# Streaming both halves of a split fp32 operand through one 512-column matmul

## The chip, the cores and the metric

One core of one Trainium2 chip runs the whole program. The metric is device time in microseconds of that core, as the median of several executions of one compiled kernel.

## What is computed

The reference takes 256 tokens of width 2048 in fp32 through one large block (three attention branches with gates, then a convolutional feed-forward layer) and two more mixers (gated linear attention, latent attention). Nearly all of the arithmetic is in products of the token activations with large weight matrices that are read once:

```python
proj = h @ w_in                                   # 2048 x (6 x 1024 + ... + 3 x 2048)
merged = (gates[:, :, 0] * (o_sb @ w_branch[0]) + gates[:, :, 1] * (o_dsa @ w_branch[1])
          + gates[:, :, 2] * (o_mem @ w_branch[2]))
x = x + merged @ w_out
u = _causal_dwconv(h2 @ w_up, conv_w, conv_b)     # 2048 x 11008
x = x + (silu(g) * val) @ w_down                  # 5504 x 2048
# second block: the same kind of products, each followed by
x = x + rms_norm(y, g_post)
```

## The kernel before, in words

TensorE has a fast fp32 format (fp32r) that keeps fewer bits than fp32. To get fp32 accuracy each operand is split into a high part (rounded) and a low part (the rest), and a product is three matmuls that accumulate: high x high, high x low, low x high. The fourth product is left out.

**Phases.** The projections are 38 phases in a fixed order (class Phase, L44; list at L200). A phase has blocks of 256 output columns, and a block has 1 to 4 tiles of weights; a tile is 4 (in one place 3) slices of 128 rows by 256 columns, 512 KB. There are 836 tiles. The kinds: "fm" keeps weights still and streams the 256 tokens, so that the output has features on partitions; "tm" keeps the activations of 128 tokens still and streams 256 weight columns; "kv" (16 blocks) does one half each way. Three phases have narrow blocks of one block each, "tm" with 72, 16 and 64 columns (kiwi, decay, krope). The phases qrope, qnope0, qnope1, kv0 and kv1 have one tile in a block, all others two or more.

**Engines.** For each tile SyncE issues the load into one of RING = 4 places of `weight_raw`; ScalarE copies it to `weight_hi` (split_hi, L1087, instruction L1092); VectorE subtracts to make `weight_lo` (split_lo, L1630, instruction L1628, the line of the helper that records every tensor-tensor operation); TensorE runs the 24 matmuls of the tile (project, L589, instruction L628) and signals `tile_used`. ScalarE splits tile t + 4 once tile t is used, so weights are ready some tiles ahead.

**PSUM.** `blk` (L295) has PSUM_RING = 2 places of two banks; a block uses columns 0 to 255 of each bank. TensorE may start block b + 2 when `block_out` says that block b has been taken out. Who takes it out: ScalarE for rows_to (L1119), chunks_to (L1133), gate_tanh (L1139, tanh straight from PSUM) and y_out (L1542); VectorE for scaled_to (L1705, times 1/rms), branch (L1873, times the gate), add_to_x (L2030), conv_scale (L2050) and the kv output (L2273). Each engine's queue is in order: per tile ScalarE does split_hi, then an output, then `mid` and `side` work (softmax, norms, convolution) that is placed by tile index; VectorE does its output first, then split_lo, then `mid` and `side`.

**After an "up" phase** the last block goes through VectorE (conv_scale), ScalarE and VectorE (taps, L1436, L2067, L2072), ScalarE (silu, L1441), VectorE (product), ScalarE (L1445, high part) and VectorE (low part `h_lo`); the "down" phase that follows needs that last chunk in its last tile of the first block: the fourth tile in down0 and down1, the third in down2.

Of the kernel before, what the change touches and what calls it, by code (L numbers as in the profile page):

```python
# [25 lines left out]
P = 128  # L26
ALU = mybir.AluOpType
ACT = mybir.ActivationFunctionType
# [15 lines left out]
class Phase:  # L44


    def __init__(self, name, kind, blocks, ktiles, cols, src):
        self.name, self.kind, self.blocks, self.ktiles = name, kind, blocks, ktiles
        self.cols, self.src = cols, src
        self.bt = len(ktiles)  # L50
        self.n = blocks * self.bt

        self.period = lcm(PSUM_RING * self.bt, RING)


class Plan:


    def __init__(self, phases):
# [3 lines left out]
        b = 0  # L63
        for ph in phases:
            ph.t0, ph.b0 = len(self.shape), b
# [51 lines left out]
S = 256  # L117
# [42 lines left out]
def build_program(nc, x, mem, positions, attn_norm, mem_norm, w_in, b_gate, dsa_q_norm, dsa_k_norm,  # L160
# [33 lines left out]
    def qrope_src(b, kt):  # L194
# [6 lines left out]
        Phase("memk", "tm", 4, K16, TC, cols_from(w_mem_kv[0], 0, K16)),  # L201
        Phase("memv", "tm", 4, K16, TC, cols_from(w_mem_kv[0], W, K16)),
        Phase("qm", "tm", 4, K16, TC, cols_from(win, 6 * W, K16)),
        Phase("gate2", "fm", 8, K16, TC, cols_from(win, GATE0 + 2 * D, K16)),
        Phase("branch2", "fm", 8, K8, TC, cols_from(w_branch[0, 2], 0, K8)),
        Phase("sbqk", "fm", 8, K16, TC, cols_from(win, 0, K16)),
        Phase("sbv", "tm", 4, K16, TC, cols_from(win, 2 * W, K16)),
        Phase("gate0", "fm", 8, K16, TC, cols_from(win, GATE0, K16)),
        Phase("branch0", "fm", 8, K8, TC, cols_from(w_branch[0, 0], 0, K8)),
        Phase("qi", "tm", 2, K16, TC, cols_from(win, 7 * W, K16)),  # L210
        Phase("kiwi", "tm", 1, K16, ID + IH, cols_from(win, 7 * W + IH * ID, K16, ID + IH)),
        Phase("qb", "tm", 4, K16, TC, cols_from(win, 3 * W, K16)),
        Phase("kb", "tm", 4, K16, TC, cols_from(win, 4 * W, K16)),
        Phase("vb", "tm", 4, K16, TC, cols_from(win, 5 * W, K16)),
        Phase("gate1", "fm", 8, K16, TC, cols_from(win, GATE0 + D, K16)),
        Phase("branch1", "fm", 8, K8, TC, cols_from(w_branch[0, 1], 0, K8)),
        Phase("wout", "fm", 8, K16, TC, cols_from(w_out[0], 0, K16)),
    ]
    FFN = [(0, 16), (16, 16), (32, KF - 32)]
    for f, (c0, nf) in enumerate(FFN):  # L220
# [3 lines left out]
            Phase(f"down{f}", "fm", 8, kts, TC, cols_from(down[f], 0, kts)),  # L224
# [3 lines left out]
        Phase("decay", "tm", 1, K16, DECAY_RANK, cols_from(gla_w_in, 3 * D, K16, DECAY_RANK)),  # L228
        Phase("glav", "tm", 8, K16, TC, cols_from(gla_w_in, D, K16)),
# [3 lines left out]
        Phase("krope", "tm", 1, K16, LR, cols_from(mla_w_in, 2 * LRANK, K16, LR)),  # L233
# [27 lines left out]
    with ExitStack() as ctx:  # L261
# [11 lines left out]
        h_hi, h_lo = (sb(n, [P, KD, S], F32R) for n in ("h_hi", "h_lo"))  # L273
        u_hi, u_lo = (sb(n, [P, KD, S], F32R) for n in ("u_hi", "u_lo"))
# [52 lines left out]
        probs, probsT = area(T, 4, TRI), area(T + 4 * TRI, 4, TRI)  # L327

# [56 lines left out]
        block_out = sem("block_out")  # L385
# [202 lines left out]
        def _(pe):  # L588
            def project(ph, x_hi, x_lo, side=None, x_wait=None, lead=None):  # L589

                def tile(j, i):
# [12 lines left out]
                    hi, lo = weight_hi[:, t % RING], weight_lo[:, t % RING]  # L604
                    for c in range(2):
                        tok = slice(c * P, c * P + P)
                        if ph.kind == "fm":
                            o = blk[:, b % PSUM_RING, c, 0:S]
                            ops = [(w[:, k, c * P:c * P + P], v[:, TK * kt + k, :])
                                   for k in range(nk) for w, v in ((hi, x_hi), (hi, x_lo), (lo, x_hi))]  # L610
                            groups = [(o, ops)]
                        elif ph.kind == "tm":
                            o = blk[:, b % PSUM_RING, c, 0:ph.cols]
                            ops = [(v[:, TK * kt + k, tok], w[:, k, 0:ph.cols])
                                   for k in range(nk) for w, v in ((hi, x_hi), (lo, x_hi), (hi, x_lo))]
                            groups = [(o, ops)]
                        elif c == 0:
                            groups = [(blk[:, b % PSUM_RING, 0, 0:S],
                                       [(w[:, k, 0:P], v[:, k, :])
# [1709 lines left out]
```

## Time and profile before

| | us |
|---|---|
| median of 3 runs (2691.66 to 2693.73) | 2693.29 |
| span of the profiled execution | 2691.4 |
| TensorE matmul busy | 2643.3 (98%) |
| TensorE weight load busy | 2610.1 (97%) |
| VectorE busy | 1535.4 (57%) |
| ScalarE busy | 1239.8 (46%) |
| GpSimd busy | 115.3 (4%) |
| HBM read | 439.02 MB, 164 GB/s |

The span runs from the first to the last instruction of the program in one profiled execution. Matmul spans in the trace overlap each other, and their ends are modelled; the distance from one start to the next is what an instruction costs. Busy shares are averages over stages that differ.

### The profile page before, as it was taken

The numbers are of one execution on the slowest core, as the hardware profiler recorded it, in microseconds if no ns is written. First come the engines' busy times: TensorE is split into PE (matmuls) and PEld (weight loads), VectorE is DVE, ScalarE is ACT, GpSimd is POOL, SyncE is SP. The second block draws the span as 40 slices with busy tenths as digits, with TensorE's granted clock in tenths as the row PEclk, the third lists the DMA queues.
The fourth block names the chain that finished last, engine by engine and source line by source line (L and its number), as shares of the span: only waits on it lengthen the run. The fifth ranks groups of instructions, "written<-read, shape, count | busy, mean of one in ns | idle before, by whom it ended". The sixth has DMA issues, their size and how long they took to land.

```text
span 2691.4 us, 53007 instructions
## 1 busy us (share of the span) xinstructions
PE 2643.3 (98%) x21308; PEld 2610.1 (97%) x21308; DVE 1535.4 (57%) x1829; ACT 1239.8 (46%) x1551; POOL 115.3 (4%) x82
## 2 busy tenths in 40 slices
PE   7999999999999999999999999999999997999998
PEld 7999999999999999999999999999999997999897
DVE  6644544554684566666466646675254846565454
ACT  6544344543444444554345434453344444334353
POOL 3000000100000001000000000010001111000001
PEclk9999999998999999999999999999899998899998
DMA  6554555454555655665566556556354553444443
GB/s 202 181 180 141 181 186 180 145 174 141 160 179 154 201 175 185 181 181 185 183 180 183 183 181 183 179 177 180 112 165 133 167 186 111 125 119 141 117 165 109
DMA packets 545539, 443.49 MB, mean 165 GB/s; under 512 B 31241, under 2 KB 542753, under 8 KB 544866
## 3 DMA queue, kind: packets, MB, share of 16 engines
q1 hardware_dynamic: 545186, 441.00, 53.5%
q8 instruction: 120, 1.97, 0.3%
q0 software_dynamic: 192, 0.18, 0.1%
q14 instruction: 41, 0.34, 0.0%
HBM read 439.02 MB, written 2.10 MB: 164 GB/s over the span
## 4 chain that ended last, share of the span: by engine, by line
PE 95%; DVE 3%; ACT 1%; DMA 0%; issue 0%; POOL 0%; SPq 0%; DVEq 0%; ACTq 0%
PE blk L628 88%; PE pa L881 1%; DVE arena L1628 1%; PE pa L692 1%; DVE u_lo L1675 1%; DVE weight_lo L1628 0%; DMA weight_raw<-in_w_mem_kv_dram 0%; PE pa L972 0%; DVE xT L1628 0%; ACT weight_hi L1092 0%; POOL arena L570 0%; PE pa L683 0%; PE pa L654 0%; DVE arena L2185 0%; PE pa L644 0%
## 5 line engine op out<-in xcount | busy, mean ns | idle before, releaser
L1628 DVE TENSOR_TENSOR weight_lo<-weight_raw,weight_hi 128x1024 fp32r<-128x1024 f32 (+2 forms) x836 | 1018.5, 1222 | 973.5 <-ACT weight_hi L1092 971.4
L1092 ACT ACTIVATE weight_hi<-weight_raw 128x1024 fp32r<-128x1024 f32 (+2 forms) x836 | 871.2, 1045 | 1283.5 <-PE blk L628 1251.2
L628 PE MATMUL blk<-u_hi,weight_hi 128*128 128x256 f32 x2656 | 756.8, 285 | 16.5 <-DVE u_lo L1675 14.4
L628 PE MATMUL blk<-u_lo,weight_hi 128*128 128x256 f32 x2656 | 754.4, 284 | 0.0
L628 PE MATMUL blk<-u_hi,weight_lo 128*128 128x256 f32 x2656 | 754.3, 284 | 0.0
L628 PE MATMUL blk<-h_hi,weight_hi 128*128 128x256 f32 x2608 | 741.9, 284 | 1.8 <-DVE h_lo L1628 1.8
L628 PE MATMUL blk<-h_hi,weight_lo 128*128 128x256 f32 x2608 | 738.7, 283 | 0.0
L628 PE MATMUL blk<-h_lo,weight_hi 128*128 128x256 f32 x2608 | 738.6, 283 | 0.0
L628 PEld LDWEIGHTS blk<-u_hi,weight_hi 128*128 128x128 f32 x2656 | 512.6, 193 | 19.3 <-issue 16.7
L628 PEld LDWEIGHTS blk<-u_lo,weight_hi 128*128 128x128 f32 x2656 | 512.8, 193 | 0.1
L628 PEld LDWEIGHTS blk<-u_hi,weight_lo 128*128 128x128 f32 x2656 | 512.7, 193 | 0.0
L628 PEld LDWEIGHTS blk<-h_hi,weight_hi 128*128 128x128 f32 x2608 | 501.3, 192 | 2.1 <-issue 2.0
L628 PEld LDWEIGHTS blk<-h_lo,weight_hi 128*128 128x128 f32 x2608 | 501.4, 192 | 0.1
L628 PEld LDWEIGHTS blk<-h_hi,weight_lo 128*128 128x128 f32 x2608 | 501.2, 192 | 0.0
L628 PE MATMUL blk<-weight_lo,h_hi 128*128 128x256 f32 (+2 forms) x896 | 257.0, 287 | 0.0
L628 PE MATMUL blk<-weight_hi,h_lo 128*128 128x256 f32 (+2 forms) x896 | 256.8, 287 | 0.0
L628 PE MATMUL blk<-weight_hi,h_hi 128*128 128x256 f32 (+2 forms) x896 | 256.6, 286 | 0.0
L628 PEld LDWEIGHTS blk<-weight_hi,h_hi 128*128 128x128 f32 x896 | 176.8, 197 | 0.5 <-DVE weight_lo L1628 0.3
L628 PEld LDWEIGHTS blk<-weight_hi,h_lo 128*128 128x128 f32 x896 | 176.8, 197 | 0.0
L628 PEld LDWEIGHTS blk<-weight_lo,h_hi 128*128 128x128 f32 x896 | 176.7, 197 | 0.0
L628 PE MATMUL blk<-weight_hi,u_hi 128*128 128x256 f32 (+2 forms) x576 | 170.5, 296 | 4.7 <-DVE weight_lo L1628 4.7
L628 PE MATMUL blk<-weight_lo,u_hi 128*128 128x256 f32 (+2 forms) x576 | 168.8, 293 | 0.0
(244 smaller groups left out, 1991.7 us busy)
## 6 DMA issues: line engine op xcount, KB each, us to landing
weight_raw<-in_w_in_dram SPq DMA_DIRECT2D x216, 512.0 KB, 3.4
weight_raw<-in_w_up_dram SPq DMA_DIRECT2D x344, 256.0 KB, 3.1
weight_raw<-in_l_gla_w_in_dram SPq DMA_DIRECT2D x96, 512.0 KB, 3.7
weight_raw<-in_w_down_dram SPq DMA_DIRECT2D x80, 512.0 KB, 3.3
weight_raw<-in_w_branch_dram SPq DMA_DIRECT2D x48, 512.0 KB, 3.3
weight_raw<-in_l_mla_w_in_dram SPq DMA_DIRECT2D x48, 512.0 KB, 3.7
weight_raw<-in_w_mem_kv_dram SPq DMA_DIRECT2D x32, 512.0 KB, 4.3
weight_raw<-in_w_out_dram SPq DMA_DIRECT2D x32, 512.0 KB, 3.3
```

What stands on the lines that cost most here:

```text
L628: mm = nc.tensor.matmul(o, lhsT, rhs, start=(kt == 0 and m == 0), stop=(kt == ph.bt - 1 and m == len(ops) - 1))
L692: nc.tensor.matmul(pa[:, h, 0:S], values[:, 0, v], probs_T[:, h, 0:S], start=True, stop=False)
L881: mm = nc.tensor.matmul(pa[:, h, o], lhsT, rhs, start=(m == 0), stop=(m == len(ops) - 1))
L1092: nc.scalar.activation(weight_hi[:, r, 0:nk, 0:cols], weight_raw[:, r, 0:nk, 0:cols], ACT.Copy).then_inc(hi_made, 1)
L1628: return nc.vector.tensor_tensor(out_, a, b, op)
L1675: nc.vector.scalar_tensor_tensor(x_lo[:, c, :], src[:, c, :], col(gain, c), x_hi[:, c, :].bitcast(F32), ALU.mult, ALU.subtract).then_inc(N ...
```

## The change

Phases with more than one tile in a block become "merged". The two halves of the streamed operand lie side by side (`weight[P, RING, 2, TK, TC]`, `h` and `u` as `[P, 2, KD, S]`), and one matmul streams both: 512 columns in two runs of 256, into columns 0 to 511 of a bank. A second matmul, with the low part of the other operand still, streams the high half into columns 0 to 255. So three matmuls of 256 columns become one of 512 and one of 256. The bank ends with two partial results in its two halves, which have to be added: ScalarE copies the upper half to SBUF ("lift", signal block_lifted), then VectorE adds the lower half from PSUM ("join", signal block_joined or block_out). Where the old output did arithmetic straight from PSUM, it now follows as its own instruction on SBUF data. `add_to_x` needs no lift: VectorE adds both halves in two instructions. Phases with one tile in a block keep their three matmuls.

```diff
+        self.merged = self.bt > 1
+        self.lift = self.merged and evict != "add"
+        self.join = self.merged and evict != "copy"
...
-        weight_hi = sb("weight_hi", [P, RING, TK, TC], F32R)
-        weight_lo = sb("weight_lo", [P, RING, TK, TC], F32R)
+        weight = sb("weight", [P, RING, 2, TK, TC], F32R)
+        weight_hi, weight_lo = weight[:, :, 0], weight[:, :, 1]
...
+            def weights_still(o, w, v):
+                n = v.shape[-1]
+                if o.shape[-1] == n:
+                    return [(o, w[:, 0, :], v[:, 0, :]), (o, w[:, 0, :], v[:, 1, :]), (o, w[:, 1, :], v[:, 0, :])]
+                return [(o, w[:, 0, :], v), (o[:, 0:n], w[:, 1, :], v[:, 0, :])]
+            def weights_move(o, v, w):
+                n = w.shape[-1]
+                if o.shape[-1] == n:
+                    return [(o, v[:, 0, :], w[:, 0, :]), (o, v[:, 0, :], w[:, 1, :]), (o, v[:, 1, :], w[:, 0, :])]
+                return [(o, v[:, 0, :], w), (o[:, 0:n], v[:, 1, :], w[:, 0, :])]
...
+                    halves = 1 + ph.merged
-                            o = blk[:, b % PSUM_RING, c, 0:S]
+                            o = blk[:, b % PSUM_RING, c, 0:halves * S]
...
 # ScalarE, in tile(), after split_hi
+                        lift(b, r).then_inc(block_lifted if ph.merged else block_out, 1)
+                        if final is not None:
+                            act.wait_ge(block_joined, b + (ph.j0 + 1))
+                            final(b).then_inc(block_out, 1)
...
+            def tanh_of_gate(g):
+                def go(b):
+                    for c in range(2):
+                        v = gates[:, bass.ds(b * 2 + c, 1), :]
+                        ins = nc.scalar.activation(v, v, ACT.Tanh, bias=col("b_gate", b * 2 + (g * KD + c)), scale=0.5)
...
 # VectorE, in tile(), after split_lo
+                    if j % ph.bt == ph.bt - 1 and join is not None:
+                        dve.wait_ge(block_lifted, b + (ph.l0 + 1))
+                        join(ph, b, r)
...
+            def chunks_joined(dst, done):
+                def go(ph, b, r):
+                    v = dst[:, bass.ds(b * 2, 2), :]
+                    tt(v, v, blk[:, r, :, 0:S], ALU.add).then_inc(done, 1)
...
 # VectorE, branch(n)
+                    v = m if n == 0 else branch_part[:, r]
+                    tt(v, v, blk[:, r, :, 0:S], ALU.add).then_inc(block_joined, 1)
+                    dve.wait_ge(block_joined, b + (ph.j0 + 1))
+                    tt(v, v, g, ALU.mult).then_inc(block_out, 1)
...
 # VectorE, add_to_x
+                    tt(v, v, blk[:, r, :, 0:S], ALU.add).then_inc(block_joined, 1)
+                    dve.wait_ge(block_joined, b + (ph.j0 + 1))
+                    tt(v, v, blk[:, r, :, S:2 * S], ALU.add).then_inc(block_out, 1)
...
 # VectorE, conv_scale
+                    v = conv_in[:, r]
+                    tt(v, v, blk[:, r, :, 0:S], ALU.add).then_inc(block_joined, 1)
+                    dve.wait_ge(block_joined, b + (ph.j0 + 1))
+                    tt(v, v, RSTD["ffn"].unsqueeze(1).to_broadcast([P, 2, S]), ALU.mult).then_inc(block_out, 1)
...
 # ScalarE, y_out
-                    unit_norm(n, b, blk[:, r, :, 0:S], 2)
+                    unit_norm(n, b, y[:, 2 * b:2 * b + 2, :], 2)
+                    norm_at(act, n, "sq", b + 1)
```

## Rows read from the trace of the kernel before

**Rows 1.** The page: busy time of TensorE, and the chain that ended last

```profile
PE 2643.3 (98%) x21308; PEld 2610.1 (97%) x21308; DVE 1535.4 (57%) x1829; ACT 1239.8 (46%) x1551; POOL 115.3 (4%) x82
PE 95%; DVE 3%; ACT 1%; DMA 0%; issue 0%; POOL 0%; SPq 0%; DVEq 0%; ACTq 0%
```

**Rows 2.** Timeline of TensorE, us 1000 to 1004: start us, duration us, instruction

```profile
1000.08 0.28 PE L628 MATMUL blk<-h_hi,weight_hi 128*128 128x256 f32 x1
1000.20 0.28 PE L628 MATMUL blk<-h_lo,weight_hi 128*128 128x256 f32 x1
...
1003.92 0.28 PE L628 MATMUL blk<-h_hi,weight_lo 128*128 128x256 f32 x1
```

**Rows 3.** Groups by shape, TensorE: instruction, count, busy us, mean ns, idle before

```profile
L628 PE MATMUL blk<-u_hi,weight_hi 128*128 128x256 f32 x2656 | 756.8, 285 | 16.5 <-DVE u_lo L1675 14.4 <-DVE weight_lo L1628 2.0
L628 PE MATMUL blk<-h_hi,weight_hi 128*128 128x256 f32 x2608 | 741.9, 284 | 1.8 <-DVE h_lo L1628 1.8
L628 PE MATMUL blk<-weight_hi,h_hi 128*128 128x256 f32 x736 | 210.7, 286 | 0.0
L628 PE MATMUL blk<-weight_hi,u_hi 128*128 128x256 f32 x512 | 149.8, 293 | 4.7 <-DVE weight_lo L1628 4.7
L628 PE MATMUL blk<-weight_hi,h_lo 128*128 128x72 f32 x32 | 11.8, 368 | 0.0
```

**Rows 4.** Timeline of TensorE in a kv block: from 256 to 128 columns

```profile
2357.63 0.22 PE L628 MATMUL blk<-weight_hi,h_hi 128*128 128x128 f32 x1
2357.69 0.28 PE L628 MATMUL blk<-weight_lo,h_hi 128*128 128x128 f32 x1
2357.81 0.27 PE L628 MATMUL blk<-weight_hi,h_lo 128*128 128x128 f32 x1
```

**Rows 5.** Timeline of TensorE in decay: 16 columns

```profile
1908.83 0.26 PE L628 MATMUL blk<-weight_hi,u_lo 128*128 128x16 f32 x1
1908.94 0.26 PE L628 MATMUL blk<-weight_hi,u_hi 128*128 128x16 f32 x1
```

**Rows 6.** Timeline of weight loads of plain fp32 matmuls with 512 columns

```profile
1927.32 0.18 PEld L948 LDWEIGHTS pa<-arena 17*128 17x128 f32 x1 [0.24 <-issue]
...
1928.61 0.18 PEld L948 LDWEIGHTS pa<-arena 17*128 17x128 f32 x1 [0.24 <-issue]
```

**Rows 7.** Low clock: timeline of TensorE, then the kiwi stage among the windows by stage (us, busy of PE, PEld, DVE, ACT, POOL, granted clock)

```profile
1931.53 0.41 PE L628 MATMUL blk<-weight_lo,u_hi 128*128 128x256 f32 x1
1931.74 0.41 PE L628 MATMUL blk<-weight_hi,u_lo 128*128 128x256 f32 x1
...
646.20:663.40 17.20, 17.20 (x98) 17.20 (x97) 4.13 (x4) 4.10 (x5) 0.00 (x0) 0.60 0.46 140
```

**Rows 8.** Groups by shape, VectorE and ScalarE: the splits and outputs from PSUM

```profile
L1628 DVE TENSOR_TENSOR weight_lo<-weight_raw,weight_hi 128x1024 fp32r<-128x1024 f32 x816 | 1006.6, 1237 | 953.5 <-ACT weight_hi L1092 951.4
L1628 DVE TENSOR_TENSOR arena<-blk,rstd 128x512 f32<-128x512 f32 x67 | 46.2, 689 | 41.7 <-PE blk L628 39.9 <-ACT small L1177 1.3 <-ACT rstd L1175 0.6
...
L1092 ACT ACTIVATE weight_hi<-weight_raw 128x1024 fp32r<-128x1024 f32 x816 | 860.1, 1057 | 1252.0 <-PE blk L628 1219.7 <-issue 15.8 <-DMA weight_raw<-in_w_mem_kv_dram 7.5
L1136 ACT ACTIVATE arena<-blk 128x512 f32 x8 | 4.7, 582 | 0.0
```

**Rows 9.** Windows by stage: kb, then branch1 (columns as in the window of rows 7)

```profile
719.20:766.90 47.70, 47.70 (x402) 47.70 (x401) 43.61 (x96) 23.55 (x25) 0.00 (x0) 1.00 0.59 179
...
920.60:966.70 46.10, 46.10 (x386) 46.10 (x385) 33.51 (x35) 20.54 (x21) 0.00 (x0) 1.00 0.63 202
```

**Rows 10.** Timeline at the end of up2: VectorE, then TensorE

```profile
1743.10 0.69 DVE L1628 TENSOR_TENSOR arena<-blk,rstd 128x512 f32<-128x512 f32 x1 [0.88 <-PE blk L628]
1745.33 0.42 DVE L1628 TENSOR_TENSOR arena<-arena 128x256 f32<-128x256 f32 x1
...
1750.60 0.36 PE L628 MATMUL blk<-h_hi,weight_hi 128*128 128x256 f32 x1 [1.78 <-DVE h_lo L1628]
```

**Rows 11.** Windows by stage: glagate, the stretch of the output norm (columns as in rows 7)

```profile
2083.00:2117.00 34.00, 32.34 (x268) 32.06 (x266) 28.58 (x29) 15.75 (x17) 6.66 (x2) 1.00 0.47 140
```

More of the change, by code:

```diff
@@ L62, in __init__ @@
         self.end_of = []
-        b = 0
+        b = lifts = joins = 0
         for ph in phases:
-            ph.t0, ph.b0 = len(self.shape), b
+            ph.t0, ph.b0, ph.l0, ph.j0 = len(self.shape), b, lifts, joins
+            lifts += ph.blocks * ph.lift
+            joins += ph.blocks * ph.join
             for j in range(ph.n):
@@ L612, in tile @@
                         elif ph.kind == "tm":
[L613 to L616, printed above, removed]
+                            o = blk[:, b % PSUM_RING, c, 0:halves * ph.cols]
+                            groups = [[op for k in range(nk) for op in weights_move(
+                                o, x[:, :, TK * kt + k, tok], w[:, :, k, 0:ph.cols])]]
@@ L626, in tile @@
-                        for o, ops in groups:
-                            for m, (lhsT, rhs) in enumerate(ops):
-                                mm = nc.tensor.matmul(o, lhsT, rhs, start=(kt == 0 and m == 0),
+                            o = blk[:, b % PSUM_RING, 0, 0:S]
+                            groups = [[op for k in range(nk) for op in weights_still(
+                                o, w[:, :, k, 0:P], x[:, :, k, :])]]
+                        else:
+                            groups = []
+                            for q in range(NT):
+                                o = blk[:, b % PSUM_RING, 1, q * P:(q + 1) * P]
+                                groups.append([op for k in range(nk) for op in weights_move(
+                                    o, x[:, :, k, q * P:q * P + P], w[:, :, k, P:2 * P])])
@@ L629, in tile @@
+                        for ops in groups:
+                            for m, (to, lhsT, rhs) in enumerate(ops):
+                                mm = nc.tensor.matmul(to, lhsT, rhs, start=(kt == 0 and m == 0),
                                                       stop=(kt == ph.bt - 1 and m == len(ops) - 1))
@@ L1403, in round_merged @@
                                      ACT.Copy).then_inc(merged_hi, 1)
[L1406 removed]
+            project(PH["branch1"], to_branch_part(2), side=lambda j: round_merged(j // 4 - 1) if j % 4 == 0 and j > 0 else None)
             round_merged(3)
@@ L2018, in side_dsa @@
                     split_out(ATT["dsa"], g, 4)
-            project(PH["gate1"], side=side_dsa, mid=gates_of(PH["gate1"]))
+            project(PH["gate1"], join=chunks_joined(gates, block_joined), side=side_dsa, mid=gates_of(PH["gate1"]))
             dve.wait_ge(gate_done, 24)
```

320 lines of the change are left out of this document (173 added, 147 removed).

## The prediction, made before the changed kernel ran

> **What bounds the kernel now.** First the page's busy rows and the chain that ended last [rows 1]: TensorE is busy for 98% of the span and holds 95% of the chain, VectorE 57% and ScalarE 46% of the span. So time is won or lost in what a matmul costs and in the few places where TensorE waits. Busy shares say nothing on what a matmul costs, because the spans overlap; the timeline does. In steady state starts are (1003.92 - 1000.08) / 32 = 0.120 us apart [rows 2]. Next question: is that 0.120 set by the columns, by the weight load, or by something fixed per matmul? The change keeps the columns (3 x 256 = 512 + 256) and takes away one weight load and one matmul of three, so it gains only what is not columns.
>
> Four rows bear on it. (a) With 16 columns the starts are 0.11 apart [rows 5]: a weight load by itself costs 0.11. (b) Going from 256 to 128 columns, the first narrow matmul gives way after 0.06, the next after 0.12, then 0.11: the first found its weights loaded and cost its columns, the later ones wait for loads [rows 4]. So 128 columns cost 0.06 and 256 cost 0.12, which looks like a rate (0.47 ns a column), where the clock of 2.4 GHz would give 0.053 and 0.107. (c) A plain fp32 matmul with 512 columns has starts (1928.61 - 1927.32) / 3 = 0.430 apart, four times 0.1075, with its load hidden [rows 6]: there a long stream carries almost nothing beside its columns. (d) At the low clock, 1.2 GHz, 256 columns cost 0.21, which is 256 / 1.2 and nothing else [rows 7]: nothing can be gained in those stretches.
>
> **The change part by part.**
>
> Wide triples. The groups by shape [rows 3] count 2656 + 2608 + 736 + 512 = 6512 triples with 256 columns. Of these qrope has 32, qnope0 and qnope1 64, kv0 and kv1 64, which keep three matmuls: 6352 change. About a hundred lie in stretches at the low clock, which follow narrow stages; I count 6250. Each costs 3 x 0.120 = 0.360 now. Afterwards the 256-column matmul is followed by the load for the 512-column one, as tight as today: 0.120. The 512-column matmul is not in the trace. From below: 0.215, half of (c), if its excess vanishes because a load of 0.11 ends in its first half. From above: 0.240, twice 0.120, if fp32r streams at the rate that (b) suggests. A fixed excess of 0.0133 per matmul would give 0.2267. The rows of its own kind of operand speak for the upper end, the load that is hidden for the lower; I take the middle, 0.228, so a triple costs 0.348 and saves 0.012. That is 6250 x 0.012 = 75 us, between 0 and 156.
>
> By the Trainium skill, page "TensorE: Matmul & The Clock Gate", section "Back-to-back issue gap", an isolated matmul costs its columns at 2.4 GHz plus 2.5 ns. By that rule a triple would cost 0.216 + 0.109 = 0.325 and the sum would lose 219 us. The trace disagrees already for what is there: 0.120 where the rule gives 0.109 [rows 2].
>
> Narrow triples. Three stages with 72, 16 and 64 columns have 32 triples each (one of them in [rows 3]). They are bound by loads, 0.11 at full clock and 0.21 at low [rows 5, 7], and each triple loses a load: 96 x 0.11 = 11 to 96 x 0.21 = 20 us. The kiwi stage averages 17.20 / 96 = 0.179 [rows 7], so 96 x 0.179 = 17, and with a little for a clock that may recover sooner as the array is fed more columns per load, 18 us.
>
> Lift and join. Per merged block ScalarE reads 128x512 from PSUM, 0.58, and VectorE adds 128x512, 0.69 [rows 8]; outputs that did arithmetic from PSUM keep their instruction, now from SBUF. There are 216 merged blocks: at most 150 us more for VectorE (57% to about 63%), less for ScalarE, which did the copy in many phases already. That is hidden as long as three covers hold. First, the PSUM ring: from the end of a block ScalarE splits (1.06) and lifts (0.58), VectorE joins (0.69) and works on (0.69), about 3.3 with signals, against a block time of 4 x 8 x 0.348 = 11.1, or 5.6 in the branch phases with two tiles. Second, VectorE's time. The kb stage is the fullest, 43.61 of 47.70 [rows 9]; four joins make it 46.5 against a stage of 46.1, and the excess of 0.4 is taken up by the weights that are split ahead. branch1 has 33.51 of 46.10 [rows 9]; eight joins make 39.0 of 44.5. Third, ScalarE: where it must wait for block_joined (gates, glaout, mlaout), the next split_hi is queued behind, and TensorE waits for that only after some three tiles, 8 us.
>
> Where cover is gone. At the end of an "up" phase the last chunk takes 1750.60 - 1743.10 = 7.5 [rows 10]. VectorE's product starts at 1745.33; now the join (0.69), the scaling (0.69) and a signal stand between split_lo and it: 1.5 later, 9.0. down0 and down1 have three tiles of cover, 3 x 2.78 = 8.3: 0.7 stall each. down2 has two, 5.6: its stall of 1.78 grows by about 1.5. Sum 3. In glagate VectorE is busy 28.58 of 34 [rows 11] and TensorE waits for weight_lo at its end, so twelve faster tiles gain nothing there (1.2) and three joins with their waits (2.6) come on top: 4. At the ends of glaout and mlaout TensorE waits for the norm of the last block, which now comes after a lift and a join: 2 x 1.3 = 2.6. For the gates and the start I add 2.4. Together 12, between 5 and 25.
>
> **Sum.** 2691.4 - 75 - 18 + 12 = 2610 for the span. The median of the runs is 1.9 above this span, so 2612.
>
> **The rivals.**
>
> Rate-bound stream: fp32r moves at 0.47 ns a column, 512 cost 0.240, a triple 0.360 as before. For it speaks that 128 cost 0.06 and 256 cost 0.12 [rows 2, 4]; against it that plain fp32 runs at its clock [rows 6]. Only narrow stages gain: -18 + 12, 2687.
>
> Hidden load: the excess comes from the load that ends together with the stream, and a long stream has none. 0.215 + 0.120 = 0.335: -156 - 18 + 14, 2533. For it rows 6, against it that the first 128-column matmul, with its weights ready, still cost 0.06 and not 0.053 [rows 4].
>
> No excess in either: the plain fp32 rate throughout, 0.215 + 0.109 = 0.325: -219 - 18 + 16, 2472. For it rows 6, against it rows 2. This is what the page's rule amounts to.
>
> Slower: reading two runs of 256 that lie apart costs extra at the seam, in every 512-column matmul. The point from which this decides is (18 - 12) / 6250 = 0.001 above 0.240, so 0.241; at 0.250 the kernel is at 2691.4 + 62 - 6 + 1.9 = 2749. No row shows a stream in two runs; that the reads are far ahead of the array speaks against it.
>
> It does not do what it says: the 512-column instruction is carried out as two of 256, each with its load. Then three matmuls a slice remain and only the additions stay: 2705. The plain fp32 matmuls with 512 columns stand whole in the trace [rows 6].
>
> **How the numbers follow.** Forecast 0.42 (its own range 2580 to 2660, from 0.220 to 0.235 for the long matmul); rate-bound 0.19; hidden load 0.20; no excess 0.08; seam 0.08; split in two 0.03. The range 2530 to 2692 holds the first three, 0.81. A measurement of this kernel can tell some 0.2%, 5.4 us, from no change. Faster: 0.42 + 0.20 + 0.08 + 0.11 of the rate-bound case, which lies at the bound, 0.81. Same: 0.08, the rest of that case. Slower: 0.08 + 0.03 = 0.11.
>
> **What would show it.** Starts in the timeline of a steady stage: 0.228 after a long matmul and 0.120 after a short one; any other split of the sum names the rival. L628 or its successor should have 6448 x 2 + 288 x 3 = 13 760 matmuls instead of 20 208. Weight loads should be busy for clearly less than 97%. The copies of 0.58 and additions of 0.69 should appear 216 times at most, with no wait of TensorE for block_out in steady stages. A stall of about 3.4 at the start of down2 and small ones in down0 and down1 should appear. The prediction is wrong if the long matmul leaves 0.220 to 0.235, or if TensorE waits in steady stages for outputs or weights, which would mean that ScalarE's wait for the join holds back the splits.

## The result and the profile after

The changed kernel takes 2644.85 us (median, 2642.61 to 2647.79) against 2692.47 for the kernel before on the same chip: ratio 0.9825, 95% interval 0.9811 to 0.9838, some 48 us faster. The forecast was 2612, a gain of 81; somewhat over half of it came (47.6). The profiled execution spans 2646.0. First the page, busy times and the chain that ended last, the lines that answer to [rows 1].

```profile
PE 2570.5 (97%) x14860; PEld 2239.3 (85%) x14860; DVE 1666.9 (63%) x2063; ACT 1310.4 (50%) x1686; POOL 107.4 (4%) x82
PE 86%; DVE 7%; ACT 4%; issue 1%; POOL 1%; DMA 1%; SPq 0%; DVEq 0%; ACTq 0%; POOLq 0%
```

TensorE still holds most of the chain, but its part fell from 95% to 86%, and VectorE and ScalarE together rose from 4% to 11%. Weight loads went from 97% to 85%. So the time is no longer only in what a matmul costs. Next the groups by shape, TensorE first, then the new copy, the new addition and the tanh that follows it, to be read against [rows 3, 8].

```profile
L648 PE MATMUL blk<-u,weight 128*128 128x512 f32 x2656 | 944.0, 401 | 17.9 <-DVE u L1752 14.5 <-DVE weight L1678 2.9 <-ACT xT L1172 0.4
...
L648 PE MATMUL blk<-u,weight 128*128 128x256 f32 x2656 | 746.6, 281 | 0.0
...
L1678 DVE TENSOR_TENSOR arena<-arena,blk 128x512 f32<-128x512 f32 x99 | 67.3, 680 | 9.4 <-ACT arena L1164 9.4
...
L1172 ACT ACTIVATE xT<-xT,vec 128x256 f32<-128x256 f32 x48 | 21.8, 502 | 34.9 <-DVE xT L1678 34.7
...
L1164 ACT ACTIVATE xT<-blk 128x512 f32<-128x512 f32 x24 | 13.9, 580 | 0.0
```

A copy is 0.580 and an addition 0.680, as costed. New is the idle time in front of the tanh: ScalarE sat 34.7 us, in 24 blocks, waiting for VectorE's addition.

What a triple (the matmuls that make one product of a slice) costs can't be read from the 401 ns, because spans overlap. ScalarE shows it: its weight split in each tile waits for TensorE to have used a tile, so in a steady stage splits are one tile (8 triples) apart. Two steady stretches of the same kernel, splits of ScalarE between 1520 and 1700 us, then between 1300 and 1480 (count, first and last start), and last the kernel before between 1300 and 1480:

```profile
L1112 ACT ACTIVATE weight<-weight_raw x65: 1042/1060/1062, 1521.4 to 1698.9; 128x1024 fp32r<-128x1024 f32 x65
...
L1112 ACT ACTIVATE weight<-weight_raw x63: 1043/1062/1063, 1300.6 to 1475.8; 128x1024 fp32r<-128x1024 f32 x63
```
```profile
L1092 ACT ACTIVATE weight_hi<-weight_raw x63: 1042/1058/1060, 1299.6 to 1478.1; 128x1024 fp32r<-128x1024 f32 x63
```

(1698.9 - 1521.4) / 64 = 2.773 us a tile, 0.3467 a triple; and (1475.8 - 1300.6) / 62 = 2.826, 0.3532 a triple. Nothing else differs: same shapes, same weights' size, no wait. The kernel before has one period, (1478.1 - 1299.6) / 62 = 2.88, 8 x 0.360. Over all steady triples of the changed kernel's trace the starts give 0.3507, with 0.2346 after a long matmul and 0.1161 after a short one. Then the windows of three stages: kiwi, gate1 and glagate (us, busy of PE, PEld, DVE, ACT, POOL, granted clock, DMA), against [rows 7] for the first, and gate1 in the kernel before.

```profile
638.65:645.71 7.06, 7.06 (x66) 7.06 (x65) 4.09 (x5) 4.11 (x5) 0.00 (x0) 1.00 0.68 192
791.87:904.83 112.96, 105.94 (x603) 92.68 (x602) 57.81 (x62) 56.05 (x91) 0.00 (x0) 0.97 0.53 158
1990.30:2102.64 112.34, 106.50 (x586) 92.03 (x585) 77.33 (x73) 56.11 (x59) 18.30 (x7) 0.97 0.51 150
```
```profile
814.74:920.64 105.90, 105.55 (x859) 104.53 (x858) 53.02 (x55) 52.24 (x84) 0.00 (x0) 1.00 0.54 169
```

kiwi went from 17.20 to 7.06 and its granted clock from 0.60 to 1.00. gate1 got longer, 105.9 to 113.0, although its matmuls got cheaper: TensorE idles for 7.0 us in it, where it idled for 0.4 before. What it waits for stands in the waits of TensorE over the whole trace (us in total, times, longest); the kernel before has 6.8 for the first of these lines, 0.9 for the line that is L712 here, 0.8 for L690, 1.8 for `h`, and no wait of 0.8 or more for L721, L833, L703 and L787.

```profile
PE blk L648 <- DVE weight L1678: 7.5, 5, 2.9
...
PE pa L712 <- ACT arena L1333: 7.0, 4, 3.1
...
PE pa L721 <- DVE arena L1678: 4.5, 2, 2.5
...
PE pa L690 <- ACT arena L1209: 4.1, 2, 2.8
PE blk L648 <- DVE h L1678: 4.1, 3, 3.3
PE pa L1017 <- POOL arena L576: 3.0, 1, 3.0
PE pa L833 <- POOL arena L532: 2.1, 1, 2.1
PE pa L703 <- DVE arena L1678: 1.7, 1, 1.7
...
PE pa L787 <- DVE arena L1678: 1.2, 1, 1.2
```

L690 and L1017 are sums for norms, `h` is the start of the down stages, and the other new ones are matmuls of the attention that run beside gate stages. The 7.0 of gate1 are both waits of L721 (4.5), transposes of the probabilities, and one of the four of L712 (2.5), their product with the values; that L712 has 7.0 in the whole trace as well is chance. Waits for weights and for a block's output stayed small: the first line is the start and glagate, where it grew from 1.9 to 2.9, and one output ends a wait, gate1's last tanh by 0.4 in branch1 (the 0.4 on L1172 in the groups above).

### The profile page after: what moved, and what is told of

The parts are those of the page before. It is cut to its first block, busy times and chain, and to the rows that moved or that the text cites. A ratio compares the mean times of both kernels' runs of the same rounds, so it can differ in the third digit from the quotient of the medians.

```text
span 2646.0 us, 40634 instructions
## 1 busy us (share of the span) xinstructions
PE 2570.5 (97%) x14860; PEld 2239.3 (85%) x14860; DVE 1666.9 (63%) x2063; ACT 1310.4 (50%) x1686; POOL 107.4 (4%) x82
## 4 chain that ended last, share of the span: by engine, by line
PE 86%; DVE 7%; ACT 4%; issue 1%; POOL 1%; DMA 1%; SPq 0%; DVEq 0%; ACTq 0%; POOLq 0%
PE blk L648 79%; DVE weight L1678 2%; DVE arena L1678 1%; PE pa L901 1%; ACT weight L1112 1%; ACT arena L1326 1%; PE pa L712 1%; DVE xT L1678 1%; DVE u L1752 1%; DMA weight_raw<-in_w_mem_kv_dram 0%; PE pa L992 0%; DMA weight_raw<-in_w_branch_dram 0%; DVE small L1915 0%; DVE arena L2278 0%; PE pa L703 0%
## 5 line engine op out<-in xcount | busy, mean ns | idle before, releaser
L1678 DVE TENSOR_TENSOR weight<-weight_raw,weight 128x1024 fp32r<-128x1024 f32 (+2 forms) x836 | 1019.5, 1224 | 828.2 <-ACT weight L1112 824.7
L1112 ACT ACTIVATE weight<-weight_raw 128x1024 fp32r<-128x1024 f32 (+2 forms) x836 | 870.4, 1045 | 1033.4 <-PE blk L648 990.6
L648 PE MATMUL blk<-u,weight 128*128 128x512 f32 x5312 | 948.5, 341 | 17.9 <-DVE u L1752 14.5
L648 PEld LDWEIGHTS blk<-u,weight 128*128 128x128 f32 x5312 | 817.2, 190 | 144.0 <-issue 18.0
L648 PE MATMUL blk<-h,weight 128*128 128x512 f32 (+1 forms) x5344 | 929.2, 335 | 4.1 <-DVE h L1678 4.1
L648 PEld LDWEIGHTS blk<-h,weight 128*128 128x128 f32 x5344 | 806.1, 189 | 117.1 <-issue 5.0
L648 PE MATMUL blk<-weight,h 128*128 128x256 f32 (+4 forms) x1952 | 312.1, 321 | 0.0
L648 PEld LDWEIGHTS blk<-weight,h 128*128 128x128 f32 x1952 | 278.4, 190 | 31.7 <-issue 0.3
L648 PE MATMUL blk<-weight,u 128*128 128x512 f32 (+5 forms) x1152 | 210.1, 344 | 4.6 <-DVE weight L1678 4.6
L648 PEld LDWEIGHTS blk<-weight,u 128*128 128x128 f32 x1152 | 181.4, 201 | 29.5 <-DVE weight L1678 5.4
L1475 ACT ACTIVATE arena<-arena,vec 128x256 f32<-128x256 f32 x86 | 46.5, 588 | 0.9 <-DVE arena L1678 0.9
L1172 ACT ACTIVATE xT<-xT,vec 128x256 f32<-128x256 f32 x48 | 21.8, 502 | 34.9 <-DVE xT L1678 34.7
```

Source lines behind the costliest of these rows:

```text
L648: mm = nc.tensor.matmul(to, lhsT, rhs, start=(kt == 0 and m == 0), stop=(kt == ph.bt - 1 and m == len(ops) - 1))
L1112: nc.scalar.activation(weight_hi[:, r, 0:nk, 0:cols], weight_raw[:, r, 0:nk, 0:cols], ACT.Copy).then_inc(hi_made, 1)
L1172: ins = nc.scalar.activation(v, v, ACT.Tanh, bias=col("b_gate", b * 2 + (g * KD + c)), scale=0.5)
L1475: nc.scalar.activation(conv[:, r, c, :], conv_in[:, r, c, :], ACT.Identity, bias=col("conv_b", b + at), scale=col("conv_w2", b + at)).then ...
L1678: return nc.vector.tensor_tensor(out_, a, b, op)
```

## The experiments

The theory at the start (T): the matmuls brought what the two periods say, and the copies and additions cost far more than the 12 us of the sum, because the attention work of ScalarE and VectorE is queued behind their waits for each other. The rival (R): the attention's chains were just hidden before, and a quicker TensorE uncovers them; the additions are innocent.

**Additions alone.** Each wide slice in three matmuls again, everything else as changed (shown for the kind with weights still; the other kind is changed alike).

```diff
-return [(o, w[:, 0, :], v), (o[:, 0:n], w[:, 1, :], v[:, 0, :])]
+return [(o[:, 0:n], w[:, 0, :], v[:, 0, :]), (o[:, n:2 * n], w[:, 0, :], v[:, 1, :]),
+        (o[:, 0:n], w[:, 1, :], v[:, 0, :])]
```

> The changed kernel with each wide slice computed by three matmuls of 256 columns again (high into the lower half, low into the upper half, weight's low part into the lower half); all copies and additions of the two halves stay. Nothing of the computation is left out. Every triple should cost 0.360 as before, so this measures what the copies and additions cost. Theory T (the copies and additions, above all ScalarE's wait for VectorE's addition, hold up the attention work that TensorE waits for; the change gave away some 33 us there): some of it shows already at the old pitch, 2705 to 2725, with TensorE waits of 2 us and more in gate1 behind the probabilities' copy. Rival R (the stages gate0, gate1 and mlagate wait for chains on ScalarE and VectorE that were just hidden before, and a quicker TensorE uncovers them; the additions themselves cost nothing): 2688 to 2700. My prediction's sum, which put 12 us on the additions at the new pitch: 2704.

Measured: 2720.67 us, ratio 1.0106 (1.0089 to 1.0123): the additions cost 28.5 us at the old pitch. That is T, and R's 2688 to 2700 falls. The waits of TensorE show the same lines (here two lines further down) while the matmuls are as slow as before:

```profile
PE pa L714 <- ACT arena L1335: 6.1, 3, 2.9
...
PE pa L723 <- DVE arena L1680: 3.1, 2, 1.8
```

**Matmuls alone.** The matmuls and the layout as changed, no copy and no addition; the outputs keep their old instructions and their old place in the tile, which on VectorE is ahead of its split. The upper half is never added, so one of the three partial products is left out of the result. (The edit is shortened to its sense.)

```diff
-lift(b, r).then_inc(block_lifted if ph.merged else block_out, 1)
+out_of_psum(b, ...).then_inc(block_out, 1)        # reads blk[:, r, :, 0:S]
-dve.wait_ge(block_lifted, b + (ph.l0 + 1))
-join(ph, b, r)
```

> The kernel before with the new matmuls alone: the high and low part of the moving operand stream in one 512-column matmul into the two halves, the outputs read the lower half with the old instructions, and nothing adds the upper half, so the products with the moving operand's low part are left out of the result. It measures what the matmuls alone bring. Theory T (the loss lies in copies and additions): 2692 - 79 = 2613 to 2620, gate1 at 102 to 104 us instead of 113, no new TensorE waits. Rival R (a quicker TensorE uncovers chains that stood just behind it): 2635 to 2645, gate1 at 108 or more. Both expect the two steady periods of 0.347 and 0.353 per triple, since no output instruction touches them; if only one period appears, the two levels come from VectorE's or ScalarE's reads of PSUM.

Measured: 2604.88 us (2596.1 to 2611.08), ratio 0.9666 (0.9640 to 0.9692). The matmuls bring 87.3 us. The window of gate1, and TensorE's wait for the probabilities over the whole trace:

```profile
781.05:884.21 103.16, 102.57 (x604) 90.19 (x603) 52.52 (x54) 51.78 (x84) 0.00 (x0) 1.00 0.58 172
```
```profile
PE pa L712 <- ACT arena L1314: 1.1, 2, 0.6
```

gate1 takes 103.16 with 0.6 us idle, and the wait is 1.1 in place of 7.0. So a quicker TensorE by itself uncovers nearly nothing. That gives 2644.85 - 2604.88 = 40.0 for the additions at the new pitch and 28.5 at the old. "The additions" are here everything that the new outputs bring, copies, additions, waits and their place behind the splits; the runs don't part these. R may keep a small part, some 11 us that arise only where both meet, but this kernel's executions lie 15 us apart, so the 11 is hardly clear of the spread. Both periods, 0.3467 and 0.3533, are in this trace too, so the readers of PSUM don't make them.

Lengths of stages, from a stage's first block matmul to that of the next, in us:

| stage | before | additions alone | matmuls alone | changed | ScalarE's order | both orders |
|---|---|---|---|---|---|---|
| gate2 | 109.4 | 112.5 | 106.6 | 110.6 | 107.1 | 107.8 |
| gate0 | 109.6 | 114.2 | 107.5 | 112.8 | 112.5 | 108.1 |
| gate1 | 105.9 | 111.5 | 103.2 | 113.0 | 109.5 | 106.7 |
| glagate | 110.5 | 113.5 | 110.9 | 112.4 | 111.9 | 112.1 |
| glaout | 103.4 | 106.3 | 101.7 | 103.7 | 102.9 | 102.9 |
| mlagate0 | 70.6 | 71.7 | 69.5 | 71.4 | 71.3 | 71.3 |
| mlagate1 | 71.9 | 75.4 | 71.0 | 75.8 | 74.8 | 75.8 |

Between "matmuls alone" and "changed" the three gate stages lose 4.0 + 5.3 + 9.8 = 19.1 and the two mlagate stages 1.9 + 4.8 = 6.7: most of the 38.3 between the two spans. The timeline of the changed kernel at the end of gate1 (start, duration, engine, instruction, idle before) shows how:

```profile
875.90 1.06 ACT L1112 ACTIVATE weight<-weight_raw 128x1024 fp32r<-128x1024 f32 x1 [5.30 <-PE blk L648]
876.86 0.58 ACT L1164 ACTIVATE xT<-blk 128x512 f32<-128x512 f32 x1
876.99 1.23 DVE L1678 TENSOR_TENSOR weight<-weight_raw,weight 128x1024 fp32r<-128x1024 f32 x1 [3.22 <-ACT weight L1112]
878.13 0.68 DVE L1678 TENSOR_TENSOR xT<-xT,blk 128x512 f32<-128x512 f32 x1
878.85 0.91 ACT L1172 ACTIVATE xT<-xT,vec 128x256 f32<-128x256 f32 x2 [1.40 <-DVE xT L1678]
879.66 1.43 ACT L1333 ACTIVATE arena<-pa 128x1536 f32<-128x1536 f32 x1
...
881.14 1.22 PE L712 MATMUL pa<-arena 128*128 128x256 f32 x2 [2.51 <-ACT arena L1333]
```

ScalarE copies the upper half, waits 1.40 for the addition, which itself stands behind VectorE's split (1.23), does the tanh, and only then copies the probabilities (L1333), for which TensorE has been waiting 2.51. It could have begun after the first copy, at 877.44, and began 2.2 us later. The wait has a tail: the window of TensorE right behind it (us, busy of PE, granted clock, DMA share, GB/s) shows a granted clock of 0.54, that is the lower of the two levels, 1.2 GHz, nearly throughout, after the engine had stood still; the matmuls alone have no such stretch in gate1, whose clock is 1.00. Not every stop has such a tail: the longer one of 3.31 at the start of down2, in the second line, left the clock at 1.00.

```profile
881.20:884.60 3.40, 3.40 (x11) 0.54 0.06 19
1715.50:1722.00 6.50, 3.19 (x19) 1.00 0.04 6
```

**ScalarE's order.** The tile's attention work (`side`) ahead of the wait and the tanh.

```diff
 lift(b, r).then_inc(...)
-if final is not None:
-    act.wait_ge(block_joined, b + (ph.j0 + 1))
-    final(b).then_inc(block_out, 1)
 ... mid, side ...
+if j % ph.bt == ph.bt - 1 and final is not None:
+    act.wait_ge(block_joined, b + (ph.j0 + 1))
+    final(b).then_inc(block_out, 1)
```

> The changed kernel with one step moved on ScalarE: at the end of a gate block the attention work of the tile (exponentials, copies of probabilities) is issued right after the copy of the upper half, and the wait for VectorE's addition and the tanh come last. Nothing of the computation is left out. Theory T (TensorE's new waits in the gate stages come from the attention work queued behind ScalarE's wait for the addition): gate1 goes from 113 to 103 to 106 us, gate0 and gate2 lose 1 to 3 us each, 2645 - 14 = 2631 (2626 to 2636). Rival R (those chains are merely uncovered by a quicker TensorE): moving the step by some 2 us changes less than 5 us, 2640 to 2645. mlagate0, mlagate1 and glagate have no such step and stay as they are under both.

Measured: 2636.01 us (2632.94 to 2646.24), 8.8 less than the changed kernel's median, at the upper end of T's range; the two kernels' executions overlap, so the stages have to decide. gate2 and gate1 lost 3.5 each, gate0 only 0.3, and gate1's 109.5 misses the 103 to 106 that T asked for. In gate1 the wait of L712 for the copy of the probabilities is gone, and the two of L721, behind VectorE, are 4.5 as before. So T holds for ScalarE's own work, and for the rest VectorE's order has to be tried: it issues its part of the attention behind its wait for ScalarE's copy.

**Both orders.** On VectorE `side` now stands ahead of the wait for block_lifted and the addition, where the stage is a gate stage or has no `mid`.

```diff
+if late and side is not None:
+    side(j + i * ph.period)
 if j % ph.bt == ph.bt - 1 and join is not None:
     dve.wait_ge(block_lifted, b + (ph.l0 + 1))
     join(ph, b, r)
 ... mid ...
-if side is not None:
+if not late and side is not None:
     side(j + i * ph.period)
```

> The changed kernel with the attention and gating work of a tile moved ahead of the halves' additions on both engines: ScalarE issues it before it waits for the addition and works on, VectorE issues it before it waits for ScalarE's copy and adds. Nothing of the computation is left out. Theory T (the additions cost time because other work that TensorE waits for is queued behind the two engines' waits for each other): the stages come near those of the matmuls alone, gate2 107, gate0 108 to 110, gate1 103 to 106, mlagate0 70, mlagate1 71 to 73; against 2645 that is 26 us less at most: 2619 to 2630. Rival W (it is the additions' own work on two filled engines, not the order): no better than with ScalarE's order alone, 2634 to 2638.

Measured: 2630.51 us (2622.42 to 2631.56), ratio 0.9762 (0.9748 to 0.9775), just above T's range and below W's. The three gate stages are now 322.6 together, against 336.4 changed and 317.3 with the matmuls alone: order alone gives back 13.8 of the 19.1 (of either number less than 1 is the mix of the two periods). The window of gate1, then what is left of the waits of L721:

```profile
785.30:892.03 106.73, 102.78 (x604) 90.29 (x601) 57.87 (x62) 55.74 (x91) 0.00 (x0) 1.00 0.56 168
```
```profile
PE pa L721 <- DVE arena L1678: 3.8, 2, 2.1
```

Its idle time is 4.0 instead of 7.0, and its clock 1.00 instead of 0.97: with the waits that are left the clock doesn't fall in gate1. The 3.8 are as good as all of those 4.0. For the longer of the two, 2.1, VectorE has the same instructions in the same order before it in both kernels: an addition and the gate's last step for one block, the next tile's split, and only then the scaling of the probabilities. This order inside a tile doesn't give that back, so W fits this rest.

Against the expectation mlagate0 stays at 71.3 and mlagate1 at 75.8. mlagate1's timeline in this kernel shows two engines that wait for each other in another place:

```profile
2503.20 1.22 DVE L1678 TENSOR_TENSOR weight<-weight_raw,weight 128x1024 fp32r<-128x1024 f32 x1
2504.34 0.68 DVE L1678 TENSOR_TENSOR arena<-arena,blk 128x512 f32<-128x512 f32 x1
...
2505.05 0.69 DVE L1678 TENSOR_TENSOR arena<-arena,rstd 128x512 f32<-128x512 f32 x1
...
2505.78 0.64 ACT L1191 ACTIVATE arena<-arena 128x512 f32<-128x512 f32 x1 [3.19 <-DVE arena L1678]
...
2509.16 1.43 ACT L1333 ACTIVATE arena<-pa 128x1536 f32<-128x1536 f32 x1
...
2510.64 1.22 PE L712 MATMUL pa<-arena 128*128 128x256 f32 x2 [3.08 <-ACT arena L1333]
```

Here the silu (L1191), which is itself side work, waits 3.19 for VectorE's addition and scaling, and the copy of the probabilities comes after it. This order of side work doesn't reach that; no other was tried.

**Gate stages in three matmuls.** gate0 to gate2, glagate and both mlagate get `merged = False` and their old output instructions.

```diff
-self.merged = self.bt > 1
+self.merged = self.bt > 1 and evict != "three"
-project(PH["glagate"], join=joined_scaled(g_gate, "pre0"), side=side_gla)
+project(PH["glagate"], scaled_to(g_gate, "pre0"), side=side_gla)
```

> The changed kernel with the stages gate0, gate1, gate2, glagate, mlagate0 and mlagate1 as before the change (three matmuls of 256 columns, old output instructions), everything else changed. Nothing of the computation is left out. By the difference of the stages between the two kernels (gate2 +1.2, gate0 +3.2, gate1 +7.1, glagate +1.9, mlagate0 +0.8, mlagate1 +3.9, which it gives back): 2645 - 18 = 2627 under both theories. If it stays at 2640 or more, the stage table does not add up, and stalls only move to the next stage.

Measured: 2633.52 us; the profiled execution spans 2628.9. The stages are back at 109.4, 110.0, 105.9, 110.5, 70.6 and 71.9, as in the kernel before. The table adds up; the median is 6 above what was expected, and the run that the trace shows 4.

**What sets the period.** Three changes to the matmuls alone, each with one execution, which serve only for the pitch: the first two stream other columns than the product needs, and none adds the upper half. The first streams two neighbouring chunks, so that the 512 columns lie side by side; the second does so with 384; the third lets the short matmul stream both halves too.

```diff
-return [(o, w[:, 0, :], v), (o[:, 0:n], w[:, 1, :], v[:, 0, :])]
+at = (TK * kt + min(k, nk - 2)) * S          # first two: flat is x as one row
+(o[:, 0:512], w[:, 0, k, ...], flat[:, at:at + 512]), (o[:, 0:S], w[:, 1, k, ...], flat[:, at:at + S])
+return [(o, w[:, 0, :], v), (o, w[:, 1, :], v)]          # third
```

> The kernel with the new matmuls alone, in which the 512 streamed columns lie side by side in SBUF (two neighbouring chunks of the high part) instead of in two runs that lie far apart. Result is meaningless: the upper half gets another product, and the last chunk of a tile streams its neighbour's columns; the number and the shapes of the matmuls are the same. No seam cost: a triple stays at 0.347 or 0.353, mean about 0.3505, one time 2596 to 2611. Rival seam (the second period, or the 0.0076 by which the long matmul exceeds 0.2267, comes from the jump between the two runs): only 0.347 or less remains, 2580 to 2590.

> As the one before, with 384 streamed columns in the long matmul instead of 512 (a part of the computation is left out). It tells a fixed excess per matmul from a rate per column: with 256 columns at 0.120 and 512 at 0.2346, fixed means 0.160 + 0.013 = 0.173, a pair at 0.293 to 0.300; 0.47 ns a column means 0.180 and a pair at 0.300 to 0.307. Time: some 6250 x 0.053 = 330 us less than the matmuls alone, 2260 to 2300, unless ScalarE or VectorE become the bound.

> The kernel with the new matmuls alone, in which the matmul with the weight's low part streams both halves too (product of the two low parts comes on top; nothing reads the upper half). All wide matmuls then have 512 columns. Fixed excess of 0.0133: 0.2267 each, a pair at 0.453. Rate of 0.47 ns a column: 0.240 each, a pair at 0.480. If the second steady period comes from the change between long and short matmuls, there should be one pitch only. Time: 2605 + 6250 x 0.103 = 3249 with the fixed excess, 3414 with the rate.

Measured: 2599.45, 2321.42 and 3240.8 us. The splits of ScalarE again, side by side first (two stretches), then 384 columns, then 512 columns in both:

```profile
L1128 ACT ACTIVATE weight<-weight_raw x65: 1042/1060/1062, 1300.0 to 1477.5; 128x1024 fp32r<-128x1024 f32 x65
...
L1128 ACT ACTIVATE weight<-weight_raw x28: 1043/1062/1063, 2060.9 to 2137.2; 128x1024 fp32r<-128x1024 f32 x28
```
```profile
L1128 ACT ACTIVATE weight<-weight_raw x65: 1058/1058/1062, 249.5 to 399.7; 128x1024 fp32r<-128x1024 f32 x65
```
```profile
L1112 ACT ACTIVATE weight<-weight_raw x50: 1059/1061/1062, 1540.7 to 1718.5; 128x1024 fp32r<-128x1024 f32 x50
```

- Side by side: 177.5 / 64 = 2.773 and 76.3 / 27 = 2.826 a tile. Both periods remain, at the same values: the jump between the two runs costs nothing.
- 384 columns: 150.2 / 64 = 2.347 a tile, 0.2934 for a long and a short one. At 2.4 GHz 640 columns are 0.2667; the rest is 2 x 0.0133. All steady stretches of this trace have this one period. (TensorE then waits more for splits, 20.2 us, so the total fell less than expected.)
- 512 in both: 177.8 / 49 = 3.629 a tile, / 16 = 0.2268 each: 512 / 2.4 = 0.2133 and 0.0135. Again one period.

So a matmul with its own weights costs its columns at 2.4 GHz plus a fixed 0.0133, at 256 (0.120) and 512 columns and, in turn with 256, at 384, and the rate of 0.47 ns a column, which would give 0.300 for 384 and 256, is out. On top of it 512 and 256 in turn have a second period, 0.0067 longer.

**Long ones together.** In each half tile the four long matmuls first, then the four short ones, everything else as changed.

```diff
+if ph.merged:
+    groups = [g[0::2] + g[1::2] for g in groups]
 for ops in groups:
```

> The changed kernel with the order of the matmuls inside a half tile changed and nothing else: the four long matmuls first, then the four short ones, instead of long and short in turn. Nothing of the computation is left out. Theory A (each matmul carries a fixed 0.0133, and the second period of 0.3533 is a way in which a strict alternation of long and short can lock; 512 columns alone go at 0.2267 and 256 alone at 0.120): every wide tile goes at 8 x 0.3467 = 2.773 us whatever came before, the mean per triple falls from 0.3507 to 0.347 and the kernel gains 6250 x 0.004 = 25 us, 2620 (2616 to 2626), with less spread between runs. Rival B (the second period belongs to a state of the machine, not to the order of the instructions): two levels per tile remain, 2638 to 2648. Rival C (a change from long to short costs something itself): below 0.3467 per triple, under 2610.

Measured: 2644.34 us (2643.77 to 2652.05), ratio 0.9819 (0.9804 to 0.9834): no gain. The splits in the two stretches where the changed kernel had its two periods:

```profile
L1114 ACT ACTIVATE weight<-weight_raw x64: 1042/1060/1067, 1299.7 to 1476.5; 128x1024 fp32r<-128x1024 f32 x64
...
L1114 ACT ACTIVATE weight<-weight_raw x65: 1042/1060/1067, 1519.3 to 1698.9; 128x1024 fp32r<-128x1024 f32 x65
```

176.8 / 63 = 179.6 / 64 = 2.806, 0.3508 a triple in both. The two periods are gone, so they do hang on the order, against B's reason though the time is B's; but the one in their place is not the 0.3467 of theory A, it lies between them. A's fixed excess therefore doesn't hold for a mixture in any order. What the extra 0.004 consists of stays open.

**Together.** The two orders of side work with the grouped order; then glagate and the mlagate stages in three on top; and that last step with the matmuls in turn.

> The grouped order together with the side work ahead of the additions on both engines. Nothing of the computation is left out. If both gains are independent (theory A above, and 14 us of the side work): 2645 - 25 - 14 = 2606 (2602 to 2612). If the faster tiles only uncover the chains in the attention stages again: 2612 to 2618.

> As the one before, and glagate, mlagate0 and mlagate1 computed in three matmuls of 256 columns with the old output instructions, since these stages took 112.1, 71.3 and 75.8 us with the additions and 110.5, 70.6 and 71.9 without them. Nothing of the computation is left out. Expected 6 us below the one before, 2600 (2595 to 2608); the rival is that their stalls, uncovered, come back elsewhere: equal to the one before.

> The kernel with the side work ahead of the additions on both engines (2630.5), in which glagate, mlagate0 and mlagate1 are computed in three matmuls of 256 columns again with the old output instructions. The matmuls stay in turn, long and short. Nothing of the computation is left out. By the stage table 1.6 + 0.7 + 3.9 = 6 us less: 2624.5 (2617 to 2628, since the steady period is 0.3467 or 0.3533 by chance of where a stage begins). With the grouped order the same step brought 5.0 us. Rival: the grouped order was what made it worth it, then 2630.

Measured: 2632.63, 2627.61 and 2625.54 us (ratio of the last 0.9759, 0.9746 to 0.9772). The step to three brought 5.0 in both settings, as the stages said (6), and the grouped order brought nothing here either (2632.63 against 2630.51), so the gain of 25 on which two of these expectations rested was not there. 2625.54 is the lowest median of a kernel that computes everything, 19 us below the changed one; from 2627.61 it can't be told apart (2621.49 to 2631.95 against 2626.39 to 2631.05).

## Why the prediction was right, and where its sum was off

2644.85 lies in the range and the sign was right; the forecast was 33 too low; the time is inside the forecast's own range of 2580 to 2660. By itself the time says little, since the range of 2530 to 2692 was wide enough for three of the cases; the case is decided by the pitch. Step by step:

- **Bound and count.** Right: only the excess over columns can be gained; 13 760 matmuls on L648; loads at 85%.
- **Wide triples.** 0.012 predicted, 360 - 350.7 = 0.0093 measured, 58 us instead of 75. The 0.228 was the middle between two bounds, not a mechanism that had been argued for; that the fixed excess, which the prediction names with 0.2267, is what the runs show (0.2268 alone; a triple 0.3467 in its better period, below the 0.348 of the sum) and lies next to that middle is in part luck. What was missing is the second period. The sign that was named, 0.228 after a long matmul and 0.120 after a short one, came as 0.2346 and 0.1161, the first just inside its 0.235; only the sum and the runs of one length show what a matmul costs. Its rivals fall by the same rows: rate-bound needs 0.240 for every long one, hidden load 0.215, the seam more for two runs than for one, and split in two would leave the pitch at 0.360. The row that was held against the last one was misread: the program has four plain fp32 matmuls with 512 columns on L948, and the trace has eight records of them, each with its own load, so they do not stand whole, and the 0.430 of [rows 6] is half of one. The pitch and the count decide against it instead. The 0.215 for 512 columns isn't touched by that.
- **The weighed rule.** The Trainium skill, page "TensorE: Matmul & The Clock Gate", section "Back-to-back issue gap", gives columns at 2.4 GHz plus 2.5 ns for an isolated matmul. No run here reaches that with weights that change every matmul: the plus is 13.3 ns at three sizes.
- **Narrow triples.** 18 predicted; kiwi, decay and krope lost 10.2 + 4.7 + 6.3 = 21.2. kiwi shows why a little more: no low clock in it, 1.00 instead of 0.60; krope still has 0.71.
- **FFN ends.** Right for down2, too high for the others. The timeline at the end of up2, to be read against [rows 10]:

```profile
1709.83 5.71 PE L648 MATMUL blk<-h,weight 128*128 128x512 f32 x32
...
1712.26 0.68 DVE L1678 TENSOR_TENSOR arena<-arena,blk 128x512 f32<-128x512 f32 x1
1712.97 0.69 DVE L1678 TENSOR_TENSOR arena<-arena,rstd 128x512 f32<-128x512 f32 x1
1713.58 0.41 DVE L1678 TENSOR_TENSOR arena<-arena 128x256 f32<-128x256 f32 x1
...
1718.85 0.47 PE L648 MATMUL blk<-h,weight 128*128 128x512 f32 x1 [3.31 <-DVE h L1678]
```

  From the block's end to down2's last group 1718.85 - 1709.83 = 9.0, as worked out; the stall is 3.31 against 3.4. The waits for `h` were 1.8 before and are 4.1 now, so down0 and down1 stall for 0.4 each, not 0.7, and the three ends add 2.3 instead of 3.
- **Added stalls.** This is the step that failed: 12 predicted, with a range up to 25, and 40.0 measured (2644.85 - 2604.88), 28.5 of it even at the old pitch. glagate was near: it gained nothing from 256 faster triples (2.4) and came 1.9 longer than before, 4.3 in all against 4. So were the ends of glaout and mlaout, 2.0 and 1.7 longer than with the matmuls alone, against 2.6 for both (from mlaout's last block matmul to the end 23.2 us against 21.5; of the 2.1 by which the stage itself is longer, 1.7 is the second period). The gates had a share in "for the gates and the start 2.4" and took 19.1; both mlagate stages had none and took 6.7. The third cover was argued wrongly: of what is queued behind ScalarE's wait for block_joined the prediction named the next split_hi, which has three tiles of slack. In the same tile, ahead of that, stands `side`, the attention's exponentials and copies, and those have almost none: in the timeline above TensorE had stood for 2.51 before the copy let it go on. The two orders of side work show it by giving 13.8 of the 19.1 back; the other 5.3, and most of what is outside the gates, stay with the additions themselves or weren't taken apart.
- **The other two covers.** They held: in kb, the fullest stage for VectorE (43.61 + 4 x 0.69 is 46.4, not 46.5), TensorE never waited and all its triples run at the longer period, 46.9 in all; in branch1 it waited 0.4 for an output.

The runs of the parts give the sum in two terms: the matmuls alone brought 87.3 where 75 + 18 = 93 were worked out, 6 missing, and the additions took 40.0 where it was 12, 28 too much. Together that is the 33.7 by which the gain fell short (81.3 - 47.6). The 87.3 is 8 more than the triples' 58 and the narrow stages' 21. Between the two traces the gain is 2691.4 - 2607.7 = 83.7, of which the narrow stages have 22.8, so that 3 are left over the triples' 58; the other 4 are that the profiled execution was 4.6 slower than the median of this kernel, whose executions lie 15 us apart.

## What to carry to other kernels

Where a new wait is put into an engine's tile, list everything that the engine issues after it in the same tile, and ask of each who waits for it and how soon: work with the least slack must stand ahead of the wait, even if it is "beside" the main work. A matmul that needs fresh weights has a fixed price beside its columns, so fewer and longer ones pay, by that price and no more; and a stage that already hides a tight chain on the other engines may be better left as it is (glagate and both mlagate stages in three brought 5.0).

## What the runs showed of the hardware that was not expected

- 512 and 256 columns in turn run at 0.3467 or at 0.3533 a triple, for hundreds of microseconds, and change over only after an interruption: in the traces of the changed kernel and of the matmuls alone every change follows a triple of at least 0.76 us from start to start. 6250 triples x 0.0067 = 42 us lie between all of one and all of the other. The kernel with the matmuls alone spread from 2596.1 to 2611.1 over four runs, where the kernel before, which has one period, spread from 2691.6 to 2693.9 over seven on that chip; that the periods cause the spread is argued, since each kernel has one trace, and the changed kernel has both periods too and spread over 5 us only.
- 512 alone, 256 alone and 384 with 256 have one period each, at the fixed excess; four 512 followed by four 256 have one at 0.3508.
- kiwi's low clock (0.60 over 17.20 us) was gone when each slice had two matmuls, 144 and 72 columns, instead of three of 72; the stage then took 7.06 us for 64 matmuls, 0.110 each. With the additions and three matmuls of 72 columns it took 15.21 us at a clock of 0.69, so it is the matmuls that did it, not the outputs.
